# Feed-forward weights stored in alternating columns, some moving operands read backwards, and two mixers' inputs interleaved

## What is computed

```python
def conv_ffn(xn, w_gate, conv_w, conv_b, w_up, w_down):
    g = xn @ w_gate                      # 1024 -> 2816
    gp = jnp.pad(g, ((0, 0), (CONV_WIDTH - 1, 0), (0, 0)))
    gc = conv_b + sum(conv_w[j] * gp[:, j:j + S] for j in range(CONV_WIDTH))
    h = jax.nn.gelu(gc, approximate=False) * (xn @ w_up)
    return h @ w_down                    # 2816 -> 1024
...
    h = h + mix.astype(h.dtype)
    f = conv_ffn(rms_norm(h, norm_ffn[i]), ffn_w_gate[i], ffn_conv_w[i], ffn_conv_b[i], ffn_w_up[i], ffn_w_down[i])
    h = h + f.astype(h.dtype)
```

## Time and profile before

| | |
|---|---|
| median of 2 runs | 1072.6 us |
| profiled execution, first to last instruction (span) | 1070.4 us |
| the median less that span | 2.2 us |
| TensorE matmuls busy | 1064.7 us, 99% |
| TensorE weight loads busy | 932.3 us, 87% |
| DVE busy | 839.0 us, 78% |
| ACT busy | 655.2 us, 61% |
| DMA, mean | 179 GB/s |

### The profile page before, as it was taken

The page is one execution under the profiler, slowest core; times in us unless marked ns, Lnnn a source line. Parts: engine busy times, 40 slices in busy tenths (PEclk is TensorE's granted clock), DMA queues, the critical chain, the costliest instruction groups (busy, mean ns, idle before and its releaser), DMA issues.

```text
span 1070.4 us, 16292 instructions
## 1 busy us (share of the span) xinstructions
PE 1064.7 (99%) x6536; PEld 932.3 (87%) x6536; DVE 839.0 (78%) x1364; ACT 655.2 (61%) x922; POOL 1.3 (0%) x8
## 2 busy tenths in 40 slices
PE   9999999999999999999999999999999999999998
PEld 7778888888898888888889888888877788888888
DVE  7985799886668779987667999876668768997852
ACT  7666567665458766765556577654456765776540
POOL 0000000000000000000000000000000000000000
PEclk9999999999999999999999999999999999999999
DMA  9552446555426155655552466455555533665540
GB/s 339 181 180 114 156 164 233 195 186 216 163 83 252 55 180 190 230 202 181 214 195 81 151 215 229 182 217 187 187 177 182 174 106 140 236 220 190 206 142 30
DMA packets 32091, 191.67 MB, mean 179 GB/s; under 512 B 4496, under 2 KB 6160, under 8 KB 12176
## 3 DMA queue, kind: packets, MB, share of 16 engines
q1 hardware_dynamic: 32016, 190.62, 50.3%
HBM read 189.56 MB, written 1.05 MB: 178 GB/s over the span
## 4 chain that ended last, share of the span: by engine, by line
PE 94%; DVE 2%; ACT 2%; issue 1%; DMA 0%; SPq 0%; DVEq 0%; ACTq 0%
PE banks L463 21%; PE TB L463 12%; PE SB L463 11%; PE banks L465 11%; PE TB L465 6%; PE SB L465 6%; PE banks L679 4%; PE banks L686 4%; PE banks L680 4%; PE banks L422 3%; PE banks L424 3%; PE banks L423 3%; PE banks L636 2%; PE TB L610 2%; PE SB L597 1%
## 5 line engine op out<-in xcount | busy, mean ns | idle before, releaser
L1712 DVE TENSOR_TENSOR wlo<-raw,whi 128x2048 fp32r<-128x2048 f32 (+2 forms) x180 | 395.8, 2201 | 78.6 <-ACT whi L1173 78.5
L1173 ACT ACTIVATE whi<-raw 128x2048 fp32r<-128x2048 f32 (+2 forms) x180 | 330.5, 1840 | 81.3 <-PE TB L465 25.6
L463 PE MATMUL banks<-xx,whi 128*128 128x512 f32 x752 | 262.2, 390 | 0.2 <-DVE wlo L1712 0.2
L465 PE MATMUL banks<-xx,wlo 128*128 128x256 f32 x752 | 212.1, 282 | 0.0
L463 PEld LDWEIGHTS banks<-xx,whi 128*128 128x128 f32 x752 | 141.2, 188 | 30.0 <-DVE wlo L1712 0.5
L465 PEld LDWEIGHTS banks<-xx,wlo 128*128 128x128 f32 x752 | 142.1, 189 | 0.0
L463 PE MATMUL TB<-xx,whi 128*128 128x512 f32 x336 | 117.8, 390 | 0.2 <-DVE xx L1717 0.2
L463 PE MATMUL SB<-xx,whi 128*128 128x512 f32 x320 | 111.8, 390 | 0.0
L465 PE MATMUL TB<-xx,wlo 128*128 128x256 f32 x336 | 94.7, 282 | 0.0
L463 PE MATMUL banks<-hx,whi 128*128 128x512 f32 x264 | 91.7, 390 | 0.0
L465 PE MATMUL SB<-xx,wlo 128*128 128x256 f32 x320 | 90.2, 282 | 0.0
(11 more groups left out here) (244 smaller groups left out, 1944.6 us busy)
## 6 DMA issues: line engine op xcount, KB each, us to landing
raw<-in_gate SPq DMA_DIRECT2D x44, 1024.0 KB, 4.7
raw<-in_up SPq DMA_DIRECT2D x44, 1024.0 KB, 4.8
raw<-in_down SPq DMA_DIRECT2D x32, 1024.0 KB, 4.8
raw<-in_down SPq DMA_DIRECT2D x16, 768.0 KB, 4.2
raw<-in_d_kq SPq DMA_DIRECT2D x8, 1024.0 KB, 5.0
raw<-in_a_kq SPq DMA_DIRECT2D x6, 1024.0 KB, 5.8
raw<-in_a_o SPq DMA_DIRECT2D x4, 1024.0 KB, 4.8
raw<-in_b_o SPq DMA_DIRECT2D x4, 1024.0 KB, 5.6
```

The source lines that it names most:

```text
L463: e.matmul(po[:, 0:512], wh[:, k, sl], a[:, kk, :, :].rearrange("p w s -> p (w s)"), start=start, stop=stop, skip_group_check=True)
L465: return e.matmul(po[:, 0:256], wl[:, k, sl], a[:, kk, 0, :], start=False, stop=stop, skip_group_check=True)
L1173: e.activation(whi[n % RING][:, 0:nk * w], raw[n % RAW][:, 0:nk * w], ACT.Copy).then_inc(s_hi, 1)
L1712: e.tensor_tensor(wlo[n % RING][:, 0:nk * w], raw[n % RAW][:, 0:nk * w], whi[n % RING][:, 0:nk * w].bitcast(F32), ALU.subtract).then_inc(s ...
```

## The change

The instructions of each engine, their order, their sizes and their waits stay as they are. Four things change, by tables with one entry for each layer or stage.

1. *Stationary step of two* (`G_FORM` for gate and up, `D_FORM` for down; "pair"). The host stores a unit's 256 columns of each k alternately: column 0 of the first half, column 0 of the second, column 1 of the first, and so on. `columns` reads the half m from element m on with a step of two (8 bytes) in place of 128 neighbours. "pair" holds for gate and up of layers 0, 1, 2 and for down of layers 0, 1, 3.
2. *From the back* (`G_BACK`, `D_BACK`; `turned`). Both matmuls of a pair read the moving operand from the last column to the first and write the bank in the same direction. It holds for gate and up of layers 2 and 3 and for down of layers 1 and 2. The triples of `last_pair` stay forward.
3. *Shifts* (`X_AT`, `H_AT`). `xx`, `hx` and `ox` get 32 more elements, and a stage's data start some elements later: `xx` 4 in F1, `hx` 2, 4, 4 and 8 in F0 to F3. By the enlarged buffers everything behind them moves by a multiple of 128 bytes.
4. *Inputs woven* (`woven`). In A and B the high and the low part of `xx` alternate element by element, so each is written, and read as a stationary operand, with a step of two. In the other stages they lie as before.

```diff
+SHIFT = 32
+X_AT = {A: 0, F0: 0, B: 0, F1: 4, POOL: 0, F2: 0, DD: 0, F3: 0}
+H_AT = {F0: 2, F1: 4, F2: 4, F3: 8}
+O_AT = {A: 0, B: 0, DD: 0}
+G_FORM = ("pair", "pair", "pair", "flat")
+D_FORM = ("pair", "pair", "flat", "pair")
+G_BACK = (False, False, True, True)
+D_BACK = (False, True, True, False)
...
+def columns(w, k, m, form):
+    if form == "flat":
+        return w[:, k, m * 128:(m + 1) * 128]
+    return w[:, k, m:256:2]
...
-        xx = sb("xx", [128, KD, 2, S], F32R)
+        xx = sb("xx", [128, KD * 2 * S + SHIFT], F32R)
...
+        def placed(buf, n, at):
+            return buf[:, at:at + n * 2 * S].rearrange("p (k w s) -> p k w s", k=n, w=2)
+
+        def woven(buf, n, at):
+            return buf[:, at:at + n * 2 * S].rearrange("p (k s w) -> p k w s", k=n, w=2)
+
+        XX = {st: (woven if st in (A, B) else placed)(xx, KD, X_AT[st]) for st in range(8)}
+        HX = {st: placed(hx, NF, H_AT[st]) for st in (F0, F1, F2, F3)}
+        OX = {st: placed(ox, KD, O_AT[st]) for st in (A, B, DD)}
...
-                sl = slice(m * 128, (m + 1) * 128)
-                e.matmul(po[:, 0:512], wh[:, k, sl], a[:, kk, :, :].rearrange("p w s -> p (w s)"), start=start,
-                         stop=stop, skip_group_check=True)
-                return e.matmul(po[:, 0:256], wl[:, k, sl], a[:, kk, 0, :], start=False, stop=stop,
-                                skip_group_check=True)
+                form = form_of(plan[n][0])
+                both, high = a[:, kk, :, :].rearrange("p w s -> p (w s)"), a[:, kk, 0, :]
+                po, ph = po[:, 0:512], po[:, 0:256]
+                if turned(plan[n][0]):
+                    both, high, po, ph = (x[:, ::-1] for x in (both, high, po, ph))
+                e.matmul(po, columns(wh, k, m, form), both, start=start, stop=stop, skip_group_check=True)
+                return e.matmul(ph, columns(wl, k, m, form), high, start=False, stop=stop, skip_group_check=True)
...
-                                last = three(b[:, 1, 0:256], wh[:, k, 128:256], wl[:, k, 128:256], hx[:, kk, 0, :],
-                                             hx[:, kk, 1, :], start, stop)
+                                form = form_of(plan[n][0])
+                                last = three(b[:, 1, 0:256], columns(wh, k, 1, form), columns(wl, k, 1, form), HX[s][:, kk, 0, :],
+                                             HX[s][:, kk, 1, :], start, stop)
...
+def lay_formed(w, form):
+    k, n = w.shape
+    v = w.reshape(k, n // 256, 2, 128)
+    if form == "pair":
+        v = v.transpose(0, 1, 3, 2)
+    return lay_units(v.reshape(k, n), 256)
```

More of the change, by code:

```diff
@@ L98, in unit_plan, with form_of, turned @@
     return plan, first
+def form_of(name):
+    if name[:2] == "up" or name[:4] in ("gate", "down"):
+        layer = int(name.split("_")[0][-1])
+        return (D_FORM if name[:4] == "down" else G_FORM)[layer]
+    return "flat"
+def turned(name):
+    if name[:2] == "up" or name[:4] in ("gate", "down"):
+        layer = int(name.split("_")[0][-1])
+        return (D_BACK if name[:4] == "down" else G_BACK)[layer]
+    return False
+def columns(w, k, m, form):
+    if form == "flat":
+        return w[:, k, m * 128:(m + 1) * 128]
+    return w[:, k, m:256:2]
 def build(nc, dram, out):
@@ L567, in ffn @@
                     for k in range(KD):
-                        last = across_wide(n + 1, bu, k, xx, k, k == 0, k == KD - 1)
+                        last = across_wide(n + 1, bu, k, XX[s], k, k == 0, k == KD - 1)
                     last.then_inc(s_used, 1)
@@ L647, in project_01 @@
                     for c in range(2):
-                        last = across(u + c, bk(s, c), k, ox, k, k == 0, k == KD - 1)
+                        last = across(u + c, bk(s, c), k, OX[s], k, k == 0, k == KD - 1)
                         if k == KD - 1:
@@ L657, in project @@
                 for k in ks:
-                    last = across_wide(u + c, out_banks(c), k, ox, k, k == 0, k == KD - 1)
+                    last = across_wide(u + c, out_banks(c), k, OX[s], k, k == 0, k == KD - 1)
                 if ks[-1] == KD - 1:
@@ L678, in high @@
                     po = slot_bank(s, i, h)[:, :]
-                    e.matmul(po, xx[:, k, 0, sl], wh[:, k % 4, :], start=k == 0, stop=False, skip_group_check=True)
-                    e.matmul(po, xx[:, k, 1, sl], wh[:, k % 4, :], start=False, stop=False, skip_group_check=True)
+                    e.matmul(po, XX[s][:, k, 0, sl], wh[:, k % 4, :], start=k == 0, stop=False, skip_group_check=True)
+                    e.matmul(po, XX[s][:, k, 1, sl], wh[:, k % 4, :], start=False, stop=False, skip_group_check=True)
                 def low(i, h, k):
@@ L685, in low @@
                     sl = slice(h * 128, (h + 1) * 128)
-                    return e.matmul(slot_bank(s, i, h)[:, :], xx[:, k, 0, sl], wl[:, k % 4, :], start=False,
+                    return e.matmul(slot_bank(s, i, h)[:, :], XX[s][:, k, 0, sl], wl[:, k % 4, :], start=False,
                                     stop=k == KD - 1, skip_group_check=True)
@@ L935, in channels @@
                         for k in range(nk):
-                            last = three(po[:, m, :], wh[:, k, sl], wl[:, k, sl], ox[:, kk + k, 0, :],
-                                         ox[:, kk + k, 1, :], m == 0 and k == 0, k == nk - 1)
+                            last = three(po[:, m, :], wh[:, k, sl], wl[:, k, sl], OX[s][:, kk + k, 0, :],
+                                         OX[s][:, kk + k, 1, :], m == 0 and k == 0, k == nk - 1)
                     return last
@@ L961, in value_block @@
                     for k in range(2):
-                        last = three(bk(s, 2 + (h if c == 0 else 0))[:, :], ox[:, 6 + k, 0, sl], ox[:, 6 + k, 1, sl], wh[:, k, :],
+                        last = three(bk(s, 2 + (h if c == 0 else 0))[:, :], OX[s][:, 6 + k, 0, sl], OX[s][:, 6 + k, 1, sl], wh[:, k, :],
                                      wl[:, k, :], k == 0, k == 1)
@@ L1515, in latent_hi @@
                     e.wait_ge(s_lt, t + 1)
-                    e.activation(ox[:, 3 + c, 0, :], LT[t % 3], ACT.Copy, scale=gain).then_inc(s_ch, 1)
+                    e.activation(OX[s][:, 3 + c, 0, :], LT[t % 3], ACT.Copy, scale=gain).then_inc(s_ch, 1)
                 def key_rope():
@@ L2152, in latent_lo @@
                     e.wait_ge(s_ch, t + 1 if t < 2 else t)
-                    e.scalar_tensor_tensor(out=ox[:, 3 + c, 1, :], in0=LT[t % 3], scalar=gain,
-                                           in1=ox[:, 3 + c, 0, :].bitcast(F32), op0=ALU.mult,
+                    e.scalar_tensor_tensor(out=OX[s][:, 3 + c, 1, :], in0=LT[t % 3], scalar=gain,
+                                           in1=OX[s][:, 3 + c, 0, :].bitcast(F32), op0=ALU.mult,
                                            op1=ALU.subtract).then_inc(s_cl, 1)
@@ L2456 @@
             layer // 2]
-        a[f"gate{layer}"] = lay_units(i[g][j], 256)
-        a[f"up{layer}"] = lay_units(i[u][j], 256)
+        a[f"gate{layer}"] = lay_formed(i[g][j], G_FORM[layer])
+        a[f"up{layer}"] = lay_formed(i[u][j], G_FORM[layer])
         for c, (k0, k1) in enumerate(((0, 1024), (1024, 2048), (2048, 2816))):
-            a[f"down{layer}_{c}"] = lay_units(i[d][j][k0:k1], 256)
+            a[f"down{layer}_{c}"] = lay_formed(i[d][j][k0:k1], D_FORM[layer])
     idx = 256 + np.arange(128)[:, None] - np.concatenate([np.arange(128), np.arange(256) - 128])[None, :]
```

46 lines of the change are left out of this document (21 added, 25 removed).

## The result

The changed kernel takes 1087.6 us (1087.56 to 1087.58, two runs) where the kernel before takes 1072.6: 15.0 us more, a ratio of 1.0139 with a 95% interval of 1.011 to 1.0168. I had forecast 1053.8.

What follows compares the result with a forecast made beforehand. It took TensorE's own matmul spacing as the bound: step two -15.2, triples -1.6 and mixers -2.0 made -18.8 us, a span of 1051.6, plus 2.2 around it, so 1053.8 us; range 1030 to 1110.

Steps and rivals of the forecast that it cites:

- What bounds the kernel: Whole span: TensorE busy 1064.7 of 1070.4 us, waits 2.4 us, so the spacing of matmul starts, 346 ns a pair, decides.
- The yardstick of 320: Feed-forward pairs: one column per clock at 2.4 GHz, so 768 columns take 320 ns, an estimate no spacing beats.
- Stationary step of two, moving forward, 15 ns less a pair: Gate and up of layers 0 and 1, down of 0 and 3: 1012 pairs, 15 ns less each, 15.2 us less.
- the 109 ns: Feed-forward pairs: the pace of 128-column weight loads, below which a 256-wide matmul can't follow; forecast to fall there from 118.
- The triples, 8 ns less each: Layers 0, 1 and 3: 198 matmuls of 256 columns reading step two go from 117 to 109 ns, 1.6 us less.
- Mixers A and B, 2.0 us less: Mixer A's 288 512-wide matmuls with woven xx take 7 ns less each, 2.0 us; B's 96 narrower ones left out.
- From the back, 0: Gate and up of layers 2 and 3, down of 1 and 2: 1012 pairs, no row favouring either sign, taken as 0.
- Shifts, 0: Starts of xx and hx moved by 2, 4 or 8 elements: only where streams start changes, counted as 0.
- The load becomes the bound: Load beside the 256-wide matmul takes over 118 ns at step two: +30 us (1103) to +152 us (1225); chance 0.13.
- Backward streams are dear: Reading xx and writing the bank backwards runs at half rate: +324 us, 1396; a tenth gives 1105; chance 0.09.
- Nothing: All stages: the 26 ns are a fixed cost of swapping weights, whatever their addresses; 1072.6 give or take 6; chance 0.20.
- full gain: All 2024 pairs: step two, back and flat backward keep streams apart, 18 ns less each, 36 us, 1034; chance 0.22.

## Why the prediction was wrong, step by step

*What bounds the kernel*: right. TensorE's spacing is the whole time, its waits 1.7 us, and the counts of matmuls by stage showed each part. The yardstick of 320 held: nothing went under 329.0.

*Stationary step of two, moving forward, 15 ns less a pair*: this is the step that failed. It stood on "If the 26 ns are meetings of the two reads, they become rare." The rows could not say that, and the experiments say no: with one loaded column the pair stays at 346.8. The 26.7 ns are 16.7 for the moving read's walk and about 10 that stay when neither walks. There was nothing for the weave to take away. In its place it costs 3 to 13 ns a pair over 346.7 when both walk, by the distance; the load's own 6 ns, measured where the moving read stands still, are nearly hidden there. So the 1012 forward pairs cost 6.6 more (704 pairs), 13.3 (154) and 4.6 (154): +7.4 us instead of -15.2. My argument that two reads at the same rate would keep apart was geometry without a row. And the 109 ns to which I let the 256-wide matmul fall came from the transposes' loads, which take 140 ns each where the feed-forward's take 188; in no stage did that matmul take less than 112. Layer 0 went up by 6.7 ns, which the prediction had named as the sign that it is wrong.

*The triples, 8 ns less each*: 2 to 6 more.

*Mixers A and B, 2.0 us less*: 0.5 more, within its interval of none. I compared A's 233 with the feed-forward's 228 as if a layout could close it; woven, A's steps stayed at 233, and the shifts of the stationary xx by 2 to 16 elements left A's and DD's median steps at 233 to 235.

*From the back, 0*: sign unknown was honest, the size is 4.4 to 4.6 ns a pair alone, 4.6 us, all from the read. With +7.4 in place of -15.2 and nothing else changed, my sum would have been +3.8: the failed step alone turns the sign, without the terms that I had put at 0.

*Shifts, 0*: 2.8 us alone. I had taken them as harmless for the very reason that in the flat form the moving read passes over every relation; the distance counts there too, by up to 6.7 ns.

*The rivals.* "The load becomes the bound" had the right sign, but at step two it is not what the changed kernel pays: the 256-wide matmul kept its spacing (117.5 against 118.3 in gate and up of layer 0), the 512-wide one grew from 228.4 to 235.9, and the loads still start with the matmuls. Where the load is the bound, from step three on and at step two beside a standing moving read, it is the load beside the 256-wide matmul, as the rival had it; but the time shows in the 512-wide one's step, so what I had named to show it (the 256-wide spacing over 118) would have missed it. "Backward streams are dear" came true at a seventieth of its half rate. "Nothing" and "full gain" are out. The time lies in the range, and within 2% as the likeliest of the three bands had it, but that is luck: it lies on the side that I gave less, and by a mechanism with the opposite sign. One sum was off: 2024 pairs by 18 ns less are 36 us, 1036 and not 1034.

*The rules.* The one of the Trainium skill on separate read ports ("TensorE: Matmul & The Clock Gate", Part 2, step 1) would have given 1072.6 and was nearer than my term; yet the runs don't bear it out in full, since a shift of 8 costs 6.5 ns beside a walking load (353.2 against 346.7) and nothing beside one that stands (346.8). The Trainium skill's note on cachelines ("SBUF — State Buffer": two hits in a line are enough) fits the loads: 188 to 194 ns at step two, over 300 at step four. It doesn't fit the moving operand, where a step of two in 4-byte elements nearly doubled the time, 680 against 347 a pair. The Trainium skill's "PSUM — Partial Sum Buffer" warns of patterns that aren't contiguous; a reversed write, in which neighbours stay neighbours, cost nothing (346.8), and no run wrote with a larger step.

What stays open: which property of the two addresses sets the 0 to 7 ns (flat) and 3 to 13 ns (step two) (hx at a shift of 16 had two values at one distance), why 64 loaded columns at a shift of 8 gave 343.6, why loops of 16 and 32 moving columns are dearer than long walks, and what the last 10 ns are. No setting with the right products beat the kernel before, so there was no faster version to run.

## What to carry to other kernels

Before an excess over the ideal rate is put down to two streams in each other's way, let one of them stand still (a broadcast operand of one column) and see whether the excess goes; it costs one kernel and would have told here that there was nothing to win. In this kernel, weights and moving operands are best read contiguously and forward; a stream's start address is a setting worth up to 2% of a dense matmul stage (353.4 against 346.7), to be measured for the very buffers in use. Where stages are alike, one kernel can carry a different setting in each, and the mean distance of the matmuls' starts resolves a tenth of a nanosecond a pair where whole times resolve a microsecond. The step that grows doesn't tell which load is late; compare when the loads start.

## What the runs showed of the hardware that I had not expected

- A float32r moving operand with a step of two elements runs at about half rate: 680 ns for 768 columns against 347; a stationary one with the same step costs 6 ns beside a standing moving read and 3 to 13 over 346.7 beside a walking one; a step of three costs 64 ns, four 120.
- A moving operand within 32 bytes is faster by 16.7 ns in 768 columns than one that walks (330.0 against 346.7), and loops of 64 and 128 bytes are slower than a long walk (360.1 and 366.5, against 346.7).
- Backward reading costs 4.5 ns a pair (351.1), backward writing nothing (346.8).
- Start addresses shifted by 8 bytes can cost 6.7 ns a pair (xx, 353.4) or none (hx, 346.7), and xx's price is gone when the load beside reads one column (346.7).
